# Expert loads issued at the last split projection, routing by token halves, the embedding product inside routing, the memory turned in one chunk

## What is computed

```python
y = sigmoid(ma) * ya + sigmoid(mb) * yb            # recurrent unit and gated linear attention
h = layer_norm_2(DEEPNORM_ALPHA * h + y @ w_out[i], ln1_g[i], ln1_b[i])
m = moe(h, ...)      # logits = h @ w_router + b_router; top 4 of 32 experts, softmax over the four;
                     # each expert: (up_h + 1) * gate_h * sigmoid(1.702 * gate_h), then @ w_down[e] + b_down[e]
h = layer_norm_2(DEEPNORM_ALPHA * h + m, ln2_g[i], ln2_b[i])
h = h + sigmoid(h @ w_ple_gate[i] + b_ple_gate[i]) * (p[i] @ w_ple[i])
```

## Time and profile before

| what | value |
|---|---|
| three timed runs, median (lowest, highest) | 2537.65 us (2536.61, 2537.88) |
| the profiled execution, its own time | 2539.67 us |
| its span, first to last instruction | 2537.9 us |
| mean granted TensorE clock | 0.982 of full |
| TensorE busy / VectorE / ScalarE / GpSimd | 2446.8 / 1101.9 / 827.2 / 217.8 us |
| transferred | 665.16 MB, mean 262 GB/s |

### The profile page before, as it was taken

The page is one execution under the profiler, slowest core; times in us unless marked ns, Lnnn a source line. Parts: engine busy times, 40 slices in busy tenths (PEclk is TensorE's granted clock), DMA queues, the critical chain, the costliest instruction groups (busy, mean ns, idle before and its releaser), DMA issues. The chain is left out here.

```text
span 2537.9 us, 36251 instructions
## 1 busy us (share of the span) xinstructions
PE 2446.8 (96%) x15029; PEld 1797.8 (71%) x15029; DVE 1101.9 (43%) x1411; ACT 827.2 (33%) x952; POOL 217.8 (9%) x101
## 2 busy tenths in 40 slices
PE   8999999999999999999999989999999999999977
PEld 8899988999999998899989944444444444444433
DVE  5457756644644867654569721112211111211122
ACT  4344344433433444443355411212221122212120
POOL 0002402200200432100111010000000000000001
PEclk9999999999999999999999979999999999999997
DMA  7565454565565545456455347999999999999980
GB/s 238 191 202 163 150 183 143 173 199 182 170 207 175 164 150 170 146 184 205 156 163 185 117 199 316 427 429 428 428 429 429 428 428 428 428 428 429 429 368 17
DMA packets 215307, 665.16 MB, mean 262 GB/s; under 512 B 9841, under 2 KB 164207, under 8 KB 190624
## 3 DMA queue, kind: packets, MB, share of 16 engines
q1 hardware_dynamic: 214912, 662.53, 68.4%
q10 hardware_dynamic: 288, 1.05, 0.1%
HBM read 662.50 MB, written 1.05 MB: 261 GB/s over the span
## 5 line engine op out<-in xcount | busy, mean ns | idle before, releaser
L592 PE MATMUL ps<-ring_halves 128*128 128x256 f32 x5984 | 757.4, 284 | 7.9 <-DVE ring_halves L1862 5.6
L592 PEld LDWEIGHTS ps<-ring_halves 128*128 128x128 f32 x5984 | 738.1, 193 | 12.0 <-DVE ring_halves L1862 6.0
L1766 DVE TENSOR_TENSOR ring_halves<-ring,ring_halves 128x2048 fp32r<-128x2048 f32 x206 | 516.0, 2513 | 367.7 <-ACT ring_halves L1299 367.5
L1299 ACT CAST ring_halves<-ring 128x2048 fp32r<-128x2048 f32 x206 | 391.3, 1903 | 280.9 <-PE ps L592 138.2
L1154 PE MATMUL ps<-ring,work 128*64 128x512 f32 x2048 | 452.8, 596 | 23.1 <-DMA ring<-in_w_up_dram 22.3
L1287 ACT COPY work<-ps 128x512 f32<-128x512 f32 x185 | 106.9, 587 | 844.8 <-PE ps L1154 391.5
L1154 PEld LDWEIGHTS ps<-ring,work 128*64 128x64 f32 x2048 | 145.8, 137 | 324.1 <-issue 269.4
L603 PE MATMUL ps<-ring_halves,work_halves 128*128 128x512 f32 x1184 | 288.5, 391 | 0.0
L2254 DVE TENSOR_SCALAR work<-work 128x128 f32<-128x128 f32 x64 | 19.3, 343 | 606.3 <-PE ps L1154 606.3
L2375 POOL TENSOR_TENSOR h<-hn,work 128x1024 f32<-128x1024 f32 x20 | 79.0, 3949 | 2106.8 <-DVE hn L1804 1066.9
L603 PEld LDWEIGHTS ps<-ring_halves,work_halves 128*128 128x128 f32 x1184 | 219.7, 188 | 44.4 <-issue 0.5
(11 more groups left out here) (260 smaller groups left out, 1744.3 us busy)
## 6 DMA issues: line engine op xcount, KB each, us to landing
ring<-in_w_up_dram SPq DMA_DIRECT2D x128, 2048.0 KB, 22.3
ring<-in_w_down_dram SPq DMA_DIRECT2D x64, 2048.0 KB, 19.4
ring<-in_w_in_dram SPq DMA_DIRECT2D x52, 1024.0 KB, 5.2
ring<-in_ffn_gate_dram SPq DMA_DIRECT2D x44, 1024.0 KB, 5.3
...
```

What stands on the lines that cost most here:

```text
L592: mm = pe.matmul(ps[:, bank, pt * T:pt * T + T], wt[:, o:o + P], x[:, k, :], start=(k == 0 and n == 0), stop=(k == DT - 1 and n == 2))
L1299: nc.scalar.copy(high_of(name)[:], ring[:, s, :]).then_inc(hi_done.add(name), 1)
L1766: v.tensor_tensor(ring_halves[s][:], ring[:, s, :], high_of(name)[:].bitcast(F32), ALU.subtract)\
```

## The change

- The memory's two halves are turned at c = 2 both, before and after the down product of chunk 1.
- `normalise_rows` normalises in two instructions of 512 columns; the transposes wait for the first, and after four blocks for the second.
- ix is multiplied on VectorE, after the low half that follows v3, not on GpSimd.
- The products with ones run before ma0, in banks 6 and 7; ScalarE's roots and VectorE's reciprocals follow there.
- SyncE loads p and w_ple into `work` after output group 3 and starts the expert loads when ma3's products are done, at slot 6.
- Router, choice and their copies run by token halves; the turn of p, four embedding products (a token half and 512 columns each) and their ScalarE copies to `PLE` lie between the routing steps.
- The down-bias product moves into the branches, behind the reading of `most`; VectorE's two clearing memsets move into the layer norm.
- At the end the turn of p and the embedding product are gone; VectorE multiplies by the copy in SBUF.

The cores of the diff (the matching turns of the memory on ScalarE and VectorE, `turned_p`, which copies bank 1 to `PTURN` ahead of the second square root, and `between`, which calls it, are left out; so is the removal of old code that is printed above):

```diff
@@ -63,6 +63,8 @@
 BDOWN, BUPROWS, ROUTER, BEFORE = R + 1024, TH + 1024, 20000, 20256
+PTOK, PTURN, PLE = AA, AA + 512, TH
+FIRST_PAIR = WH
@@ -538,16 +541,19 @@
             wdn = a["w_down_2"].rearrange("a e (j p r) n -> p (a e) j (r n)", p=P, r=4)
-            slot_used(sp, "w2o3")
-            pos[0], size[0] = 0, RING
+            sp.wait_ge(pe_full.sem, pe_full.at(("O", "g", 3)))
+            sp.dma_start(w(PTOK, 512, "p (t n) -> p t n", t=TT),
+                         a["p_2"].rearrange("l a (t p) n -> p (l a t) n", p=P)).then_inc(ple_in.add("ptok"), 16)
+            sp.dma_start(w(V, 2048, "p (k n) -> p k n", k=2), rows(a["w_ple_2"].rearrange("a k n -> (a k) n"), 0))\
+                .then_inc(ple_in.add("wple"), 16)
+            slot_used(sp, "ma3")
+            pos[0], size[0] = FIRST_PAIR, RING
...
             ln_params(("B",), a["ln2_g_2"], a["ln2_b_2"])
-            load("ptok", a["p_2"].rearrange("l a (t p) n -> p (l a t) n", p=P), "p (t n) -> p t n", t=TT)
-            load("wple", rows(a["w_ple_2"].rearrange("a k n -> (a k) n"), 0), "p (k n) -> p k n", k=2)
@@ -631,6 +637,10 @@
                 for k in range(DT):
+                    if tag != ("x",) and k == 0:
+                        pe.wait_ge(dve_done.sem, dve_done.at(("hn half", tag, t)))
+                    if tag != ("x",) and k == 4:
+                        normed(tag, t)
@@ -655,7 +665,6 @@
                         if (i, kk) == (2, 1):
-                            normed(tag, 0)
@@ -682,7 +691,6 @@
                 half(b_name, b_bank, 0, (0,))
-                normed(tag, 1)
@@ -726,21 +734,23 @@
+                def turn_memory(t):
+                    s = arrived("mem")
+                    b = 2 - 2 * t
+                    open_bank(b, ("T", "mem", t))
+                    open_bank(b + 1, ("T", "mem", t))
+                    for k in range(DT):
+                        mm = pe.transpose(ps[:, b + k // 4, (k % 4) * P:(k % 4) * P + P],
+                                          ring[:, s, t * D + k * P:t * D + k * P + P], ident[:])
+                    if t == 0:
+                        full(mm, ("T", "mem", 0))
+                    else:
+                        release(mm, "mem")
...
                     gate_up(c)
-                    if opening and c in (2, 3):
...
+                    if opening and c == 2:
+                        turn_memory(0)
@@ -753,6 +763,8 @@
                     by_rows((tag, "down", c - 1), hid(c - 1), start=(c == 1), opening=("acc", tag) if c == 1 else None)
+                    if opening and c == 2:
+                        turn_memory(1)
@@ -1000,17 +1012,17 @@
             by_columns("ga3", 1)
-            by_columns("ma0", 0)
-            by_columns("ma1", 1)
             for j in range(2):
-                open_bank(j, ("ms", "g", j))
+                open_bank(6 + j, ("ms", "g", j))
...
                         u = 2 * (2 * j + hh) + uu
-                        mm = pe.matmul(ps[:, j, hh * T:hh * T + T], ones[:], work[:, PR + u * T:PR + u * T + T],
+                        mm = pe.matmul(ps[:, 6 + j, hh * T:hh * T + T], ones[:], work[:, PR + u * T:PR + u * T + T],
...
                 full(mm, ("ms", "g", j))
+            by_columns("ma0", 0)
+            by_columns("ma1", 1)
@@ -1042,51 +1054,76 @@
                     if (j, kk) == (3, 1):
-                        normed(after, 0)
...
                 release(mm, f"w2o{j}")
-            normed(after, 1)
+            def router(t):
+                turned_copied(after, t)
+                open_bank(2 * t, ("router", t))
+                pe.matmul(ps[:, 2 * t, 0:32], ones[0:1, :], brout[0:1, :], start=True, stop=False)
+                for k in range(DT):
+                    mm = pe.matmul(ps[:, 2 * t, 0:32], hT[:, k, t * P:t * P + P], w(ROUTER + k * 32, 32),
+                                   start=False, stop=(k == DT - 1))
+                full(mm, ("router", t))
+            def embedding(t, half):
+                b = 4 + 2 * t + half
+                open_bank(b, ("ple", t, half))
+                for kk in range(2):
+                    mm = pe.matmul(ps[:, b, :], w(PTURN + kk * T + t * P, P),
+                                   w(V + kk * D + half * 512, 512), start=(kk == 0), stop=(kk == 1))
+                full(mm, ("ple", t, half))
+            pe.wait_ge(ple_in.sem, ple_in.at("wple"))
+            turned_copied(after, 0)
+            open_bank(1, "ptok")
+            for t in range(TT):
+                for kt in range(2):
+                    mm = pe.transpose(ps[:, 1, kt * T + t * P:kt * T + t * P + P],
+                                      w(PTOK + t * 256 + kt * P, P), ident[:])
+            full(mm, "ptok")
+            pe.wait_ge(tables.sem, tables.at("all"))
+            router(0)
+            evacuated(1, "ptok")
+            embedding(0, 0)
             transposes(after, 1, hn)
-            turned_copied(after, 0)
...
+            embedding(0, 1)
+            router(1)
+            open_bank(3, "bup")
             for r in range(4):
-                mm = pe.transpose(ps[:, 1, r * P:r * P + P], work[:, bass.ds(BUPROWS + r, P, step=4)], ident[:])
+                mm = pe.transpose(ps[:, 3, r * P:r * P + P], work[:, bass.ds(BUPROWS + r, P, step=4)], ident[:])
...
-            open_bank(3, "pos")
+            embedding(1, 0)
+            open_bank(0, "pos")
...
             before = w(BEFORE, P)
-            for o, terms in ((0, [(before, chosen[0])]), (32, [(ones[:], chosen[0]), (before, chosen[1])]),
-                             (64, [(ones[:], chosen[0]), (ones[:], chosen[1])])):
+            for o, terms in ((64, [(ones[:], chosen[0]), (ones[:], chosen[1])]), (0, [(before, chosen[0])]),
+                             (32, [(ones[:], chosen[0]), (before, chosen[1])])):
                 for i, (lhs, rhs) in enumerate(terms):
-                    mm = pe.matmul(ps[:, 3, o:o + 32], lhs, rhs, start=(i == 0), stop=(i == len(terms) - 1))
+                    mm = pe.matmul(ps[:, 0, o:o + 32], lhs, rhs, start=(i == 0), stop=(i == len(terms) - 1))
             full(mm, "pos")
+            embedding(1, 1)
...
             full(mm, "gT")
-            evacuated(2, "gT")
...
+            def expert_biases(branch):
+                evacuated(2, "gT")
+                for t in range(TT):
+                    for half in range(2):
+                        open_bank(4 + 2 * t + half, ("bd", branch))
+                        mm = pe.matmul(ps[:, 4 + 2 * t + half, :], work[0:32, GT + t * P:GT + t * P + P],
+                                       work[0:32, BDOWN + half * 512:BDOWN + half * 512 + 512], start=True, stop=True)
+                full(mm, ("bd", branch))
@@ -1244,14 +1283,6 @@
-            open_bank(0, "ptok")
...
@@ -1262,16 +1293,6 @@
                 whole_rows(f"pg{j}", lambda kk, t: hT[:, 2 * j + kk, t * P:t * P + P], False, j == 3)
-            s = arrived("wple")
...
@@ -1648,26 +1679,34 @@
             through_r("ga", 3, ACT.Gelu_apprx_tanh)
+            roots([("ms", "g", j) for j in range(2)], 256, 0, 6)
...
             through_r("ma", 1, ACT.Sigmoid)
-            roots([("ms", "g", j) for j in range(2)], 256, 0)
...
             root_table()
-            ln(("A",), ("ln1_g_2", "ln1_b_2"), 0)
-            act.wait_ge(dve_done.sem, dve_done.at("rmax"))
+            ln(("A",), ("ln1_g_2", "ln1_b_2"), 0, turned_p)
             for t in range(TT):
-                ins = nc.scalar.activation(work[:, GATES + t * 32:GATES + t * 32 + 32],
...
+                act.wait_ge(dve_done.sem, dve_done.at(("rmax", t)))
+                done(nc.scalar.activation(work[:, GATES + t * 32:GATES + t * 32 + 32],
+                                          work[:, LOGIT + t * 32:LOGIT + t * 32 + 32], ACT.Exp,
+                                          bias=small[:, 40 + t:41 + t]), ("rexp", t))
             pe_group("bup")
-            nc.scalar.copy(w(BUP, 512, "p (i r) -> p r i", r=4), ps[:, 1, :].rearrange("p (r i) -> p r i", r=4))\
-                .then_inc(emptied[1].sem, 1)
+            nc.scalar.copy(w(BUP, 512, "p (i r) -> p r i", r=4), ps[:, 3, :].rearrange("p (r i) -> p r i", r=4))\
+                .then_inc(emptied[3].sem, 1)
+            def embedded(t, half):
+                pe_group(("ple", t, half))
+                copy_out(4 + 2 * t + half, w(PLE + t * D + half * 512, 512))
+            embedded(0, 0)
+            embedded(0, 1)
+            embedded(1, 0)
...
             nc.scalar.copy(work[0:32, GT:GT + T], ps[0:32, 2, 0:T]).then_inc(emptied[2].sem, 1)
+            embedded(1, 1)
@@ -1801,10 +1838,12 @@
                 link(v.reciprocal(rstd[:, t:t + 1], rstd[:, t:t + 1]))
-                done(v.tensor_scalar(hn[:, t, :], hn[:, t, :], mv[:, t, 0:1], rstd[:, t:t + 1],
-                                     ALU.subtract, ALU.mult), ("hn", tag, t))
-            def ln(tag, gname, i, alpha):
+                for half in range(2):
+                    x = hn[:, t, half * 512:half * 512 + 512]
```

(59 more changed lines are left out.)

144 lines of the change are left out of this document (40 added, 104 removed).

## The result

| | kernel before | changed kernel |
|---|---|---|
| median | 2537.34 us | 2508.57 us |
| lowest and highest | 2536.61 to 2537.88 | 2507.34 to 2508.65 |
| the profiled execution, its span | 2539.67, 2537.9 | 2508.65, 2506.9 |

The ratio of the times is 0.9883, 95% interval 0.9871 to 0.9895: 28.8 us less by the medians, 31.0 by the two spans. The forecast was 2500 with a range of 2491 to 2510, so the time lies 1.4 us inside the upper edge.

The account below looks back on a forecast made before the run. The expert loop's load queue was taken as the bound, its end tied to its restart at the seventh load. Gains of 8.1 + 2.8 + 0.7 + 15.3 + 11.1 = 38.0 us gave 2500, range 2491 to 2510.

Parts of the forecast that it names:

- a sign of being wrong: TensorE waiting over 2 us between projection and bias product, or an unkept distance from restart to last up load.
- the rivals: Five other outcomes: clock up throughout (chance 0.17), clock down early (0.20), slow branch (0.10), new wait (0.05), slower kernel (0.03).
- seventh load, 905 us, last wait: Expert loop: about 905 us from the seventh weight load's issue to TensorE's last wait for an up load, unchanged.
- the earlier loads: Before the expert loop: 8 MB of expert weights start some 30 us earlier, worth nothing alone.
- Memory turn: Opening: the slot for up load 4 frees earlier, removing a 5.61 us TensorE wait and 2.48 us of slower products; 8.1 us.
- Halves: Eight layer norms: the first transposes need only half the normalised rows, 0.35 us gained each; 2.8 us.
- ix on VectorE: Decay stage: moving the multiply off GpSimd ends contention, but a later TensorE wait grows; net 0.7 us.
- Roots: Before the output projection: earlier reciprocals start it 2.5 us sooner, and the clock staying up gives 1.9; together 4.4 us.
- Routing: From routing's first turns to the seventh load: work by token halves fills waits and keeps the clock up; 10.9 us.
- the second rival: Routing: the clock falls already at router half 1, seventh load only 5.6 us earlier, 2509.5; chance 0.20.
- The third rival: Routing: TensorE's exposed branch takes 5.5 us, not 1.2, so 4.3 worse, 2504; chance 0.10.
- The end: After the expert loop: p's turn gone gives 4.8 us, the embedding product gone 6.4; 11.1 us taken.

Follow-up runs that it names:

- its three variants: The kernel before with one part alone: the memory turn 2528.9 us, the roots a stage earlier 2533.81 us, the normalised rows in halves 2533.47 us.

## Why the prediction was right, and where it was not

The sign and the range held; the forecast was 8.6 us too low, and the order of the gains did not hold (routing was to be almost as large as the end, 10.9 and 11.1; it was 4.5 and 12.2). What the prediction had named as a sign of being wrong, a wait of TensorE over 2 us between the projection and the bias product, did appear, with 4.32 us. That the time still lies in the range is owed to the allowance for the rivals, and in part to luck: the decay stage and the end gave 1.3 and 1.1 us more than forecast.

- **The bound.** The chain "seventh load, 905 us, last wait" held in every kernel: 905.37 after, 905.53 before, and 905.0 to 906.1 in the twelve others. That the moment of the restart is the whole price of what stands ahead of the loop is shown, as is the worth of the earlier loads, nothing.
- **Memory turn**, 8.1: measured 8.3, alone and in the change.
- **Halves**, 2.8: measured 1.4 by the waits, 1.6 to 1.7 by the starts. The mis-sized step is "0.81 us is cut to between 0.41 and about 0.5": a half takes 0.54 us and the pair 1.00. An instruction of half the columns was priced at half the time, though the row in hand was one of a single size.
- **ix on VectorE**, 0.7: measured 2.0. The wait grew as foreseen (0.73 and 2.62 us for 1.64), and the 1.5 us taken back for the clock were not lost: both blocks behind ran in 5.99 and 6.00 us.
- **Roots**, 4.4: measured 4.2, alone and in the change. The 2.5 of the wait are the edit's. The 1.9 for the clock, measured 1.7, are in part luck: in two of three kernels that keep the wait of 3.0 us the clock did not fall either.
- **Routing.** This is the step that failed: 10.9 predicted, 4.5 measured. The sum put "half 0's choice (1.9)" ahead of VectorE's share of the copy. It took 5.0, because GpSimd's residual of the second half, which starts at the same event as the choice, holds the cast and the compare. In the kernel before, the choice came when GpSimd was long done, so its 2.85 us held no such cost; but I had costed one case of this contention in the decay stage and did not ask the same of the step that moved. The gap of 1 us became 4.3. So the second rival came true in its kind (the clock falls at router half 1), for another reason and not all the way, since the clock came back for 1495 to 1503.
- **Branch.** The third rival, 2504, fell: TensorE enters its branch with no more than the 0.45 us for ScalarE's copy that it waited before too, and products put ahead of it change nothing. The Trainium skill's rule (Runtime: NRT & Kernel Launch, Instruction fetch mechanics) had given the same rival. No stall of that kind stands at the entry in any trace here; at the exit there are 6.8 us that could be one.
- **The end**, 11.1: 12.2 between the two profiled executions. The kernel before took 96.2 us there, its three variants 93.8, 95.1 and 95.0; the changed one 84.0. By the mean of the four the gain is 11.0; the six kernels with other routing and the same end took 84.0 to 85.6, so 84.0 is at the short side. The prediction's "83, not 94" misread the profile before, which has 96.2; less 11.1 that is 85.1. Of the two terms, 4.8 came as forecast (from the copy of the sums to the second x, 9.8 and 5.0 us), and 6.4 became 7.3, with 1.2 us of a gate product that ran in 29.23 us instead of 30.45. GpSimd stands in VectorE's way for 2.0 us in the changed kernel (3.03 instead of 1.00), but that is no new loss: in the kernel before the same residual cost 2.1 us one operation earlier (3.43 instead of 1.29), and this row stood in the prediction's own without a question.
- **Slower by instruction fetch behind the loads:** nothing of it appeared.
